# Low parts of the recurrence's weight slots: made by VectorE in whole slots instead of by GpSimd in pieces

## The chip, the cores and the metric

The kernel runs on one core of one Trainium2 chip. The metric is the device time of one execution in microseconds (us). Five engines matter here: TensorE (PE; its weight loads are listed apart as PEld), VectorE (DVE), ScalarE (ACT), GpSimd (POOL) and SyncE (SP), which issues most of the DMA.

## What is computed

The reference is one inference step of a decoder trunk of two layers over 512 prompt tokens and 8 sample tokens, all in fp32, with 1024 channels. Of a layer, this is what matters here:

```python
x = x + 0.5 * mod[:, :, 2] * _swiglu(pre(x, 0), ...)           # first FFN half step
h = pre(x, 1)
(u_pool, hq, hf, hi, hg, aq, ak, av, iq, ik, iw, gl) = _split_in(h @ P['w_in'][l])
ya, pool_new = _pool_mix(u_pool, ...)                          # branch A
f = lb + (1.0 - lb) * jax.nn.sigmoid(hf)
o_b, s_new = _hgrn_scan(hq, log(max(f, F_FLOOR)), 1.0 - f, hi, hgrn_prev[l])   # branch B, 4 heads of 128 x 64
yc = _dsa(q, qi, iw, pos, k_all, v_all, ki_all, n_sel)         # branch C, sparse attention
x = x + mod[:, :, 5] * (merged @ P['w_out'][l])
x = x + 0.5 * mod[:, :, 8] * _swiglu(pre(x, 2), ...)           # second FFN half step
```

Branch B is a gated linear recurrence. The kernel computes it exactly, per head, by a doubling scheme over blocks of 1, 2, 4 ... 128 tokens.

## The kernel before, in words

**Products in three parts.** Every fp32 weight product is made of three matmuls: a tensor is split into a high part (fp32r) and a low part (tensor minus high part), and `product` (L1863 to L1865) and `token_tile` (L2019 to L2021) issue high x high, low x high and high x low.

**Weight slots.** The weights arrive in slots of 128 x 2048 values (1 MB). There are two sets of buffers, j = 0 and 1; slot n uses set n % 2. Per slot SP loads `raw[j]` as soon as the low part of the slot two before it is made (it waits on `w_split[j]`; `load_mix`, L701). ScalarE copies `raw[j]` to `w_hi[j]` once TensorE is through with slot n - 2 (`head`, L877, which raises `head_split[j]`). Then GpSimd makes `w_lo[j] = raw[j] - w_hi[j]` in four pieces of 128 x 512 (`split`, L820), and the last piece raises `w_split[j]`. TensorE waits on `w_split[j]` before the slot's first matmul (`wait_slot`). GpSimd does this for every slot of the kernel, in order.

**The stage "mix".** After the first FFN half step each layer has a stage of twelve slots, in the order `u, hi, H0, aq0, H1, iq, H2, aq1, H3, kv, thin, hg` (the list `MIX`). H0 to H3 hold the query and forget weights of the recurrence's four heads; the others are the projections of the other branches, whose products TensorE does between the recurrence's own small steps. The stage `ga0` (gates) follows; GpSimd makes its slots too.

**The recurrence (`hgrn`, on TensorE, VectorE and ScalarE).** For each head hd = 0 to 3 there are eight levels n = 0 to 7 (`LEVELS` = 0, 1, 2, 4 ... 64). TensorE does, for each n: first one group of 24 matmuls of a weight slot as filling, then the level's eight small matmuls (L2165), for which it waits on `pair_ready`. The filling is, at n = 1 to 4, groups of the slot `BESIDE[hd]` (aq0, iq, aq1, kv); at n = 5 to 7 and ahead of the turned keys (`kbT`, L2178), the four groups of the next head's slot H(hd+1). In head 3 the slot `thin` is the filling at n = 5 and 6, and the slot `hg` at n = 7, ahead of `kbT` and after it.

VectorE does in `hgrn` per head: `start`, `finish` of the head before, `sample_columns`, `scores(hd, 0)`, and then for n = 0 to 6: `double(hd, n)`, which waits for level n + 1 of TensorE and scales `hk` (L1531) and `qm` (L1532; this one raises `pair_ready` for level n + 2, and after n = 6 for `kbT`) and `ends` (L1534); `scores(hd, n + 1)` (four masked copies, L1551) while n + 1 < 6; and for hd > 0 one step of the rotary embedding of the slot `BESIDE[hd - 1]` (`rotary_step`): step 0 is a sum (L1448), 1 and 2 are half-width products (L645, L647), 3 is a product of 1280 columns (L649), 4 a sum of 1280 columns (L651); steps 5 and 6 are empty. The order of VectorE's instructions is written out by hand; it waits in order.

In the code below `use`/`slot_use` number the slots, `link` makes VectorE wait for its own last instruction, and the level matmuls of TensorE are in `hgrn` under `@block.tensor`.

Of the kernel before, what the change touches and what calls it, by code (L numbers as in the profile page):

```python
# [23 lines left out]
F32 = mybir.dt.float32  # L24
# [4 lines left out]
ALU = mybir.AluOpType  # L29
# [78 lines left out]

MIX = ("u", "hi", "H0", "aq0", "H1", "iq", "H2", "aq1", "H3", "kv", "thin", "hg")
BESIDE = ("aq0", "iq", "aq1", "kv")  # L110
MIX_SOURCE = {n: SLOT0["token"] + i for i, n in enumerate(("u", "hi", "hg", "aq0", "aq1", "kv", "iq", "thin"))}
MIX_SOURCE.update({f"H{hd}": SLOT0["hgrn"] + hd for hd in range(HH)})
MIX_UNIT, _at = {}, 0
# [79 lines left out]
def x_updates(sub):  # L193

    return X_TILES * (sub // N_SUB) + (0, 2 * KT, 3 * KT)[sub % N_SUB]
# [100 lines left out]
def build(nc, d):  # L296

    ctx = ExitStack()
    with ctx:
# [3 lines left out]
        def sb(name, shape, dt=F32, at=None):  # L303
            size = 4 * int(np.prod(shape[1:]))
            if at is None:
                at = cursor[0]
                cursor[0] += -(-size // 32) * 32
            assert at + size <= 229368, (name, at + size)
            return nc.alloc_sbuf_tensor_at(name, list(shape), dt, offset=at)
# [6 lines left out]
        raw = [sb(f"raw{j}", [P, SLOT]) for j in range(2)]  # L316
        w_hi = [sb(f"w_hi{j}", [P, SLOT], F32R) for j in range(2)]
        w_lo = [sb(f"w_lo{j}", [P, SLOT], F32R) for j in range(2)]
# [156 lines left out]
        def sem(name):  # L475
            return ctx.enter_context(nc.semaphore(name))
# [6 lines left out]
        head_split = [sem(f"head_split{j}") for j in range(2)]  # L483
        w_split = [sem(f"w_split{j}") for j in range(2)]
# [96 lines left out]
        def slot_use(l, stage, r=0):  # L581

            return (LAYER_STREAM * l + STREAM0[stage]) // 2 + r
# [5 lines left out]
        def mix_unit(l, name, n=0):  # L589

            return main_unit(l, "mix", MIX_UNIT[name] + n)
# [5 lines left out]
        def wait_unit_taken(eng, unit):  # L597
            eng.wait_ge(main_taken[unit % 4], unit // 4 + 1 + PRIMED)
# [58 lines left out]
        def _(sp):  # L657
# [40 lines left out]
            def load_mix(l, slot):  # L698
                j = slot % 2
                sp.wait_ge(w_split[j], slot_use(l, "mix", slot // 2) + PRIMED)  # L700
                sp.dma_start(raw[j][:], d["w"][l * LAYER_SLOTS + MIX_SOURCE[MIX[slot]]]).then_inc(w_loaded[j], 16)  # L701

# [103 lines left out]
        @block.gpsimd  # L806
        def _(pool):
            for semaphore in primed:
                pool.sem_inc(semaphore, PRIMED)
            pool.memset(ones[:], 1.0).then_inc(setup_done, 1)  # L810
            pool.memset(h_hi[:, :, COLS:].bitcast(F32), 0.0).then_inc(setup_done, 1)
            pool.memset(h_lo[:, :, COLS:].bitcast(F32), 0.0).then_inc(setup_done, 1)

            def split(l, stage, r, j):
                n = COLUMNS[stage]

                pool.wait_ge(head_split[j], slot_use(l, stage, r) + 1)
                for first in range(0, n, SPLIT_PIECE):
                    cols = slice(first, min(n, first + SPLIT_PIECE))
                    last = pool.tensor_tensor(w_lo[j][:, cols], raw[j][:, cols], w_hi[j][:, cols].bitcast(F32),  # L820
                                              ALU.subtract)
                last.then_inc(w_split[j], 1)

            def square(sub, k):

                before = SQUARES * sub + 2 * k - 1
                if sub == 0:
                    if k == 0:
                        pool.wait_ge(x_loaded, 32)
                else:  # L830
                    pool.wait_ge(x_updated, x_updates(sub) - KT + k + 1)
                if k == 0:
                    pool.tensor_tensor(sq_sum[:], x[:, 0, :], x[:, 0, :], ALU.mult).then_inc(squared, 1)
                else:
                    pool.wait_ge(squared, before)
                    pool.tensor_tensor(sq[:], x[:, k, :], x[:, k, :], ALU.mult).then_inc(squared, 1)
                    pool.wait_ge(squared, before + 1)
                    pool.tensor_tensor(sq_sum[:], sq_sum[:], sq[:], ALU.add).then_inc(squared, 1)

            for k in range(KT):  # L840
                square(0, k)
            for l in range(DEPTH):
                for stage, slots, _ in STREAM:
                    sub = N_SUB * l + {"down01": 1, "out": 2, "down11": 3}.get(stage, 0)
                    if sub == N_SUB * l or sub == N_SUB * DEPTH:
                        with pool.Fori(0, slots // 2) as r:
                            for j in range(2):
                                split(l, stage, r, j)
                        continue
                    per = KT // slots  # L850
                    for slot in range(slots + 2):
                        if slot < slots:
                            split(l, stage, slot // 2, slot % 2)
                        for k in range(per * (slot - 2), per * (slot - 1)):
                            if k >= 0:
                                square(sub, k)
# [3 lines left out]
        def _(act):  # L860
# [207 lines left out]
            def hgrn(l):  # L1068
# [10 lines left out]
                act.wait_ge(pool_stored, 48 * (l + 1))  # L1079
                for hd, name in enumerate(BESIDE):  # L1080
                    if hd > 0:
# [192 lines left out]
        def _(dve):  # L1274
            v = nc.vector
# [3 lines left out]
            def bc(ap, shape):  # L1279
                return ap.to_broadcast(shape)  # L1280
# [164 lines left out]
            def square_sums(l, name, n, sq_):  # L1445
                dve.wait_ge(rot_squared, 4 * l + n)
                rows = rows_of[name] if name != "ki" else slice(14, 15)
                v.reduce_sum(rot_ms[:, 0, :, rows], sq_, axis=AX.X).then_inc(rot_reduced, 1)  # L1448

            def rotary_step(l, name, step):  # L1450

                if step == 0:
                    for u in range(3):
                        wait_unit_taken(dve, mix_unit(l, name, u))
                    if name != "iq":
                        square_sums(l, name, 1 if name == "aq0" else 2, rot_sq[:])
                else:
                    rotate(steps, step - 1, rot[:, :, rows_of[name], :], rot_tmp[:], rope if name == "iq" else rope_q)
# [37 lines left out]
            def hgrn(l):  # L1496
# [19 lines left out]
                def sample_columns(hd):  # L1516
# [2 lines left out]
                    v.tensor_copy(k_s[:, hd, :], hk[hd % 2][:, SEQ:COLS])  # L1519
                    link(v.tensor_copy(q_s[:, hd, :], hq[hd % 2][:, SEQ:COLS]))  # L1520

                def double(hd, n):


                    h = LEVELS[n + 1]
                    dve.wait_ge(side_full, SIDE[(l, "level", hd, h)] + 1)
                    m = SEQ // (2 * h)
                    ev = ends[n][:].rearrange("p (m a) -> p m a", a=2)
                    kv_ = hk[hd % 2][:, 0:SEQ].rearrange("p (m a h) -> p m a h", a=2, h=h)[:, :, 0, :]
                    qv = qm[hd % 2][:].rearrange("p (m a h) -> p m a h", a=2, h=h)[:, :, 1, :]  # L1530
                    v.tensor_tensor(kv_, kv_, bc(ev[:, :, 1:2], [P, m, h]), ALU.mult)  # L1531
                    v.tensor_tensor(qv, qv, bc(ev[:, :, 0:1], [P, m, h]), ALU.mult).then_inc(pair_ready, 1)  # L1532
                    pairs[0] += 1
                    link(v.tensor_tensor(ends[n + 1][:], ev[:, :, 0], ev[:, :, 1], ALU.mult))  # L1534
# [36 lines left out]
                for hd in range(HH):  # L1571
                    start(hd)
                    if hd > 0:
                        finish(hd - 1)
                    sample_columns(hd)
                    scores(hd, 0)
                    for n in range(len(LEVELS) - 1):
                        double(hd, n)
                        if n + 1 < MASKED:
                            scores(hd, n + 1)  # L1580
                        if hd > 0:
                            rotary_step(l, BESIDE[hd - 1], n)
                    link(v.tensor_copy(decay[:, hd % 2], ends[-1][:]))
                square_sums(l, "kv", 3, rot_sq[:, :, 0:2, :])
                finish(HH - 1)
# [260 lines left out]
        def _(pe):  # L1846
# [283 lines left out]
            def hgrn(l):  # L2130
# [18 lines left out]
                for hd in range(HH):  # L2149
                    for n, h in enumerate(LEVELS):  # L2150
                        if 1 <= n < 5 and hd + n > 1:
                            token_group(l, BESIDE[hd], n)
                        elif n >= 5 and hd + 1 < HH:
# [26 lines left out]
                    if hd + 1 < HH:  # L2180
                        token_group(l, BESIDE[hd + 1], 0)
                    else:
# [247 lines left out]
            for l in range(DEPTH):  # L2430
                for f in range(2):
# [7 lines left out]
                    if f == 0:  # L2439
# [6 lines left out]
                        pool_branch(l)  # L2446
                        token_group(l, BESIDE[0], 0)
                        pool_products(l)
                        token_group(l, BESIDE[0], 1)
                        hgrn(l)  # L2450
# [134 lines left out]
```

## Time and profile before

| | us |
|---|---|
| median of 3 runs | 2930.19 |
| lowest, highest run | 2920.36, 2930.44 |
| the profiled execution | 2916.29 |
| its span | 2914.5 |
| mean granted TensorE clock, share of 2.4 GHz | 0.967 |
| busy: TensorE, VectorE, ScalarE, GpSimd | 2740.3, 990.0, 817.3, 1116.9 |
| recurrence of layer 0, from the first level to the last head's `kbT` | about 551 to 695 |
| recurrence of layer 1 | about 1991 to 2135 |

The rows further down have times in us from the start of the span, unless they are marked ns. Busy times of TensorE are of pipelined matmuls, so a busy stretch says that it had work, not how fast that was: the pitch, the distance from one start to the next, says how fast. In a timeline each row has the start, the duration (of several instructions merged, from the first start to the last end), engine, line, operation, output<-inputs and shapes, the count, and in square brackets the idle time before it and what ended it.

### The profile page before, as it was taken

Reading aid. Unit: us, or ns where it says so; the run is one execution under the profiler, and the core shown is the slowest. Engines: PE = TensorE matmul, PEld = TensorE weight load, DVE = VectorE, ACT = ScalarE, POOL = GpSimd, SP = SyncE. Lnnn points to the kernel's source line nnn. Section 1 sums busy time; section 2 is a strip of 40 time slices with the busy share of each in tenths; the row PEclk is TensorE's granted clock in tenths of the full one; section 3 lists DMA queues with packets and bytes.
Section 4 is the critical chain, followed back from the end, with each engine's and each line's share of the span. In section 5 each row is a group of like instructions: output and inputs, shape, how many; then the busy total and the mean of one; then the engine's idle time right before and its main releaser. Section 6 shows DMA issues by size and latency. Waiting matters only on the chain.

```text
span 2914.5 us, 53187 instructions
## 1 busy us (share of the span) xinstructions
PE 2740.3 (94%) x21968; PEld 2576.9 (88%) x21968; DVE 990.0 (34%) x2372; ACT 817.3 (28%) x1250; POOL 1116.9 (38%) x897
## 2 busy tenths in 40 slices
PE   5999998999989989999979999989999899799998
PEld 2999997999878879999979999979988789799998
DVE  2111113267584441112131111134666844421121
ACT  1321222322344223212233212122233332232221
POOL 4434344333212254344444444442342123544443
PEclk7999998999999989999989999989999999899999
DMA  7334435212212223342224344441122122222322
GB/s 275 130 128 174 149 109 183 73 59 77 86 33 77 103 84 128 126 156 87 78 97 149 122 168 140 144 160 59 59 83 73 32 86 102 73 87 80 108 76 83
DMA packets 75223, 312.78 MB, mean 107 GB/s; under 512 B 14940, under 2 KB 25594, under 8 KB 57610
## 3 DMA queue, kind: packets, MB, share of 16 engines
q1 hardware_dynamic: 67394, 290.85, 29.3%
q10 hardware_dynamic: 7640, 19.17, 1.8%
q8 instruction: 147, 2.41, 0.3%
q14 instruction: 42, 0.34, 0.0%
HBM read 299.56 MB, written 10.66 MB: 106 GB/s over the span
## 4 chain that ended last, share of the span: by engine, by line
PE 89%; DVE 6%; issue 2%; ACT 1%; DMA 1%; SPq 0%; POOL 0%; DVEq 0%; ACTq 0%; POOLq 0%
PE bank L1863 23%; PE bank L1865 21%; PE bank L1864 21%; PE bank L2019 2%; PE bank L2020 2%; PE bank L2021 2%; PE bank L1897 2%; PE bank L2165 2%; PE bank L1931 2%; PE bank L1932 2%; PE bank L1933 2%; DMA ada_w<-in_ada 1%; PE bank L2285 1%; PE bank L2298 1%; DVE score L1649 1%
## 5 line engine op out<-in xcount | busy, mean ns | idle before, releaser
L820 POOL TENSOR_TENSOR w_lo<-raw,w_hi 128x512 fp32r<-128x512 f32 (+1 forms) x800 | 1010.6, 1295 | 1730.3 <-ACT w_hi L877 1730.3
L1863 PE MATMUL bank<-h_hi,w_hi 128*128 128x260 f32 x3744 | 1074.7, 287 | 3.5 <-ACT silu_g L913 3.5
L1864 PE MATMUL bank<-h_hi,w_lo 128*128 128x260 f32 x3744 | 1059.5, 283 | 0.0
L1865 PE MATMUL bank<-h_lo,w_hi 128*128 128x260 f32 x3744 | 1059.3, 283 | 0.0
L1863 PEld LDWEIGHTS bank<-h_hi,w_hi 128*128 128x128 f32 x3744 | 709.6, 190 | 54.7 <-issue 53.3
L1864 PEld LDWEIGHTS bank<-h_hi,w_lo 128*128 128x128 f32 x3744 | 709.8, 190 | 0.0
L1865 PEld LDWEIGHTS bank<-h_lo,w_hi 128*128 128x128 f32 x3744 | 709.5, 190 | 0.0
L877 ACT CAST w_hi<-raw 128x2048 fp32r<-128x2048 f32 (+3 forms) x220 | 377.9, 1718 | 547.5 <-PE bank L1865 472.2
L1863 PE MATMUL bank<-mid_hi,w_hi 128*128 128x260 f32 x1408 | 403.6, 287 | 9.8 <-DVE mid_lo L1379 9.8
L1865 PE MATMUL bank<-mid_lo,w_hi 128*128 128x260 f32 x1408 | 398.1, 283 | 0.0
L1864 PE MATMUL bank<-mid_hi,w_lo 128*128 128x260 f32 x1408 | 396.6, 282 | 0.0
L1374 DVE TENSOR_TENSOR prod<-silu_g,bank 128x260 f32<-128x260 f32 x176 | 74.9, 425 | 732.0 <-PE bank L1865 709.0
L1863 PEld LDWEIGHTS bank<-mid_hi,w_hi 128*128 128x128 f32 x1408 | 264.3, 188 | 30.3 <-issue 25.2
L1865 PEld LDWEIGHTS bank<-mid_lo,w_hi 128*128 128x128 f32 x1408 | 265.7, 189 | 0.0
L1864 PEld LDWEIGHTS bank<-mid_hi,w_lo 128*128 128x128 f32 x1408 | 265.4, 188 | 0.0
L916 ACT CAST mid_hi<-prod 128x260 f32 (+1 forms) x176 | 72.1, 410 | 487.0 <-DVE prod L1374 487.0
L1413 DVE SCALAR_TENSOR_TENSOR x<-bank,mod,x 128x260 f32 (+3 forms) x160 | 77.5, 485 | 296.2 <-PE bank L1865 248.1
L2019 PE MATMUL bank<-w_hi,h_hi 128*128 128x256 f32 x560 | 166.2, 297 | 7.9 <-DVE h_lo L1339 7.9
L2020 PE MATMUL bank<-w_hi,h_lo 128*128 128x256 f32 x560 | 161.7, 289 | 0.0
L2021 PE MATMUL bank<-w_lo,h_hi 128*128 128x256 f32 x560 | 161.6, 289 | 0.0
L1379 DVE TENSOR_TENSOR mid_lo<-prod,mid_hi 128x260 f32 (+1 forms) x176 | 102.6, 583 | 117.2 <-ACT mid_hi L916 117.2
L913 ACT ACTIVATE silu_g<-bank 128x260 f32<-128x260 f32 x176 | 68.2, 387 | 200.4 <-PE bank L1865 198.9
(321 smaller groups left out, 3224.5 us busy)
## 6 DMA issues: line engine op xcount, KB each, us to landing
raw<-in_w SPq DMA_DIRECT2D x120, 1024.0 KB, 4.9
ada_w<-in_ada SPq DMA_DIRECT2D x86, 768.0 KB, 4.4
raw<-in_w SPq DMA_DIRECT2D x64, 512.0 KB, 4.4
raw<-in_w SPq DMA_DIRECT2D x32, 768.0 KB, 4.5
raw<-in_w SPq DMA_DIRECT2D x32, 640.0 KB, 4.0
ada_first<-in_ada SPq DMA_DIRECT2D x10, 768.0 KB, 13.6
out_y<-x ACTq DMA_DIRECT2D x4, 1040.0 KB, 5.5
x<-out_y ACTq DMA_DIRECT2D x4, 1040.0 KB, 6.2
```

What stands on the lines that cost most here:

```text
L820: last = pool.tensor_tensor(w_lo[j][:, cols], raw[j][:, cols], w_hi[j][:, cols].bitcast(F32), ALU.subtract)
L877: s.copy(w_hi[j][:, 0:n], raw[j][:, 0:n]).then_inc(head_split[j], 1)
L916: s.copy(mid_hi[:, bass.ds(2 * r + j, 1), half(hf)].rearrange("p o n -> p (o n)"), prod[:, hf, :]).then_inc(mid_hi_ready, 1)
L1374: v.tensor_tensor(prod[:, hf, :], silu_g[:, hf, :], bank[2 * hf + 1][:, 0:HALF], ALU.mult).then_inc(main_taken[2 * hf + 1], 1)
L1379: v.tensor_tensor(mid_lo[:, at, half(hf)].rearrange("p o n -> p (o n)"), prod[:, hf, :], mid_hi[:, at, half(hf)].rearrange("p o n -> p (o ...
L1413: v.scalar_tensor_tensor(out=xs, in0=bank[b][:, 0:cols.stop - cols.start], scalar=md[:, bass.ds(at + 16, 1), 0:1].rearrange("p o c -> p (o ...
L1863: mm(out, wh(wb), xh(xb), start=(n == 0), stop=False)
L1864: mm(out, wl(wb), xh(xb), start=False, stop=False)
L1865: last = mm(out, wh(wb), xl(xb), start=False, stop=(n == len(blocks) - 1))
L2019: mm(out, h_hi[:, k, cols], w_hi[j][:, wcols], start=(k == 0), stop=False)
L2020: mm(out, h_lo[:, k, cols], w_hi[j][:, wcols], start=False, stop=False)
L2021: return mm(out, h_hi[:, k, cols], w_lo[j][:, wcols], start=False, stop=(k == KT - 1))
```

## The change

A constant `VECTOR_SPLITS = 4` is added. GpSimd makes the low parts of the first four slots of `mix` (u, hi, H0, aq0) as before, in pieces. The other eight (H1, iq, H2, aq1, H3, kv, thin, hg) are made by VectorE, each with one instruction of 128 x 2048: in head hd, slot 4 + 2 hd after the scores of n = 1, and slot 5 + 2 hd after `double` of n = 5. The rotary steps 0 to 4, which stood at n = 0 to 4, now stand at n = 0, 2, 3, 4 and 6.

```diff
+VECTOR_SPLITS = 4
...
             for l in range(DEPTH):
                 for stage, slots, _ in STREAM:
+                    if stage == "mix":
+                        for slot in range(VECTOR_SPLITS):
+                            split(l, stage, slot // 2, slot % 2)
+                        continue
                     sub = N_SUB * l + {"down01": 1, "out": 2, "down11": 3}.get(stage, 0)
...
+                def split(slot):
+
+                    j = slot % 2
+                    dve.wait_ge(head_split[j], slot_use(l, "mix", slot // 2) + 1)
+                    v.tensor_tensor(w_lo[j][:], raw[j][:], w_hi[j][:].bitcast(F32), ALU.subtract).then_inc(w_split[j], 1)
+
...
                         if n + 1 < MASKED:
                             scores(hd, n + 1)
-                        if hd > 0:
-                            rotary_step(l, BESIDE[hd - 1], n)
+                        if hd > 0 and n in (0, 2, 3, 4, 6):
+                            rotary_step(l, BESIDE[hd - 1], (0, 2, 3, 4, 6).index(n))
+                        if n in (1, 5):
+                            split(VECTOR_SPLITS + 2 * hd + n // 5)
```

## Rows read from the trace of the kernel before

**Rows 1.** The page: busy times, and the chain that ended last by engine.

```profile
PE 2740.3 (94%) x21968; PEld 2576.9 (88%) x21968; DVE 990.0 (34%) x2372; ACT 817.3 (28%) x1250; POOL 1116.9 (38%) x897
PE 89%; DVE 6%; issue 2%; ACT 1%; DMA 1%; SPq 0%; POOL 0%; DVEq 0%; ACTq 0%; POOLq 0%
```

**Rows 2.** Windows: one per head, layer 0; the last row head 3, layer 1.

```profile
core 0: us, PE busy (x) PEld busy (x) DVE busy (x) ACT busy (x) POOL busy (x), PEclk, DMA share, GB/s
553.00:586.00 33.00, 32.63 (x280) 32.47 (x280) 17.20 (x53) 8.64 (x13) 10.22 (x8) 1.00 0.10 33
586.00:623.00 37.00, 36.21 (x305) 35.69 (x305) 25.14 (x61) 8.43 (x14) 11.44 (x9) 1.00 0.17 58
623.00:661.00 38.00, 37.13 (x313) 36.61 (x313) 24.88 (x61) 9.79 (x16) 12.46 (x9) 1.00 0.16 56
661.00:698.00 37.00, 34.64 (x279) 34.14 (x277) 25.19 (x52) 10.20 (x19) 13.14 (x9) 0.95 0.26 87
...
2101.00:2138.00 37.00, 34.63 (x278) 34.12 (x278) 25.39 (x52) 10.37 (x19) 13.35 (x9) 0.95 0.28 87
```

**Rows 3.** Waits of TensorE, 550 to 712 us: total, times, longest.

```profile
PE bank L2165 <- DVE qm L1532: 3.3, 4, 1.9
PE bank L2141 <- issue: 1.1, 3, 0.4
```

**Rows 4.** Timeline of TensorE, head 3 of layer 0.

```profile
674.84 1.05 PE L2165 MATMUL bank<-qm,hk 128*128 128x128 f32 x8
...
678.59 1.05 PE L2165 MATMUL bank<-qm,hk 128*128 128x128 f32 x8
679.40 0.36 PE L1863 MATMUL bank<-h_hi,w_hi 128*68 128x260 f32 x1
...
683.01 1.13 PE L2165 MATMUL bank<-qm,hk 128*128 128x128 f32 x8 [0.49 <-DVE qm L1532]
684.05 0.39 PE L2019 MATMUL bank<-w_hi,h_hi 128*128 128x256 f32 x1
...
689.06 1.13 PE L2165 MATMUL bank<-qm,hk 128*128 128x128 f32 x8 [1.87 <-DVE qm L1532]
...
690.17 0.42 PE L2020 MATMUL bank<-w_hi,h_lo 128*128 128x256 f32 x1
...
693.38 0.35 PE L2020 MATMUL bank<-w_hi,h_lo 128*128 128x256 f32 x1
...
694.40 0.60 PE L2178 MATMUL bank<-ident,hk 128*128 128x128 f32 x4
```

**Rows 5.** Timeline of VectorE, head 3 of layer 0.

```profile
676.00 0.43 DVE L1531 TENSOR_TENSOR hk<-hk,ends 128x256 f32<-128x256 f32 x1 [1.48 <-PE bank L2165]
676.34 0.42 DVE L1532 TENSOR_TENSOR qm<-qm,ends 128x256 f32<-128x256 f32 x1
...
676.89 0.62 DVE L1551 COPY_PREDICATED att<-levels,bank 128x64 f32<-128x64 uint32 x4
677.43 2.57 DVE L649 TENSOR_TENSOR rot<-rot,rope_q 128x1280 f32<-128x1280 f32 x1
680.03 1.40 DVE L1531 TENSOR_TENSOR hk<-hk,ends 128x256 f32<-128x256 f32 x1
681.35 1.51 DVE L1532 TENSOR_TENSOR qm<-qm,ends 128x256 f32<-128x256 f32 x1
...
684.59 1.48 DVE L651 TENSOR_TENSOR rot<-rot,rot_tmp 128x1280 f32<-128x1280 f32 x1
```

**Rows 6.** Timeline of GpSimd: the slots aq1, hg and the first of `ga0`.

```profile
602.60 6.63 POOL L820 TENSOR_TENSOR w_lo<-raw,w_hi 128x512 fp32r<-128x512 f32 x4 [16.26 <-ACT w_hi L877]
...
677.36 6.64 POOL L820 TENSOR_TENSOR w_lo<-raw,w_hi 128x512 fp32r<-128x512 f32 x4 [16.32 <-ACT w_hi L877]
684.81 6.47 POOL L820 TENSOR_TENSOR w_lo<-raw,w_hi 128x512 fp32r<-128x512 f32 x4 [0.81 <-ACT w_hi L877]
```

**Rows 7.** Timeline of ScalarE: the high parts of `hg` and of `ga0`'s first slot.

```profile
675.36 1.92 ACT L877 CAST w_hi<-raw 128x2048 fp32r<-128x2048 f32 x1
...
682.83 1.90 ACT L877 CAST w_hi<-raw 128x2048 fp32r<-128x2048 f32 x1
```

**Rows 8.** One line of the program, L1513: ns minimum/median/maximum, first and last start.

```profile
L1513 DVE TENSOR_TENSOR qm<-hq,ends x8: 691/692/694, 551.6 to 2095.7; 128x512 f32<-128x512 f32 x8
```

**Rows 9.** Timeline of GpSimd: the slot H1, with VectorE idle beside it.

```profile
539.07 4.95 POOL L820 TENSOR_TENSOR w_lo<-raw,w_hi 128x512 fp32r<-128x512 f32 x4 [6.36 <-ACT w_hi L877]
```

**Rows 10.** DMA issues: KB each, median us from issue to landing.

```profile
raw<-in_w SPq DMA_DIRECT2D x120, 1024.0 KB, 4.9
```

**Rows 11.** Timeline of TensorE after the norm ahead of `mix`.

```profile
494.34 0.55 PE L2019 MATMUL bank<-w_hi,h_hi 128*128 128x256 f32 x1 [3.93 <-DVE h_lo L1339]
...
498.96 0.29 PE L2019 MATMUL bank<-w_hi,h_hi 128*128 128x256 f32 x1
```

## The prediction

> **What bounds the kernel now.** I read the page first: TensorE is busy 94% of the span and makes 89% of the chain that ended last, VectorE 6% [rows 1]. So a change on VectorE and GpSimd is worth only what TensorE's idle time and slow clock in the recurrence allow. Next come the windows, one per head. TensorE is busy 32.63 of 33, 36.21 of 37, 37.13 of 38 and 34.64 of 37 us; only in head 3 is its mean granted clock below full (0.95), and layer 1 repeats it (34.63 of 37, 0.95) [rows 2]. Summed, 4.4 us are idle per layer. The waits say on whom: 3.3 us in four waits on VectorE's `qm` (L1532), which releases a level, and 1.1 us in three waits for the chain of states, which the change does not touch [rows 3]. The waits of layer 1 read the same.
>
> The timelines say why. An undisturbed step from level to level takes 678.59 - 674.84 = 3.75 us: the level holds TensorE 679.40 - 678.59 = 0.81 us, the group of 24 matmuls 2.94 us [rows 4]. VectorE's `hk` starts 676.00 - 674.84 = 1.16 us after the level did. While GpSimd makes `hg` (677.36 to 684.00) and then `ga0`'s first slot (from 684.81) [rows 6], VectorE's steps stretch: `hk` from 0.43 to 1.40, `qm` from 0.42 to 1.51, the 1280-wide product takes 2.57 where a sum of that size takes 1.48 beside a gap of GpSimd [rows 5]. GpSimd pays too: 6.63 us for a slot [rows 6] against 4.95 with VectorE idle [rows 9]. Heads 1 and 2 have the same picture on a smaller scale (602.60 is head 1's).
>
> **What that costs now.** Head 3: from level 5 at 678.59, two steps to level 7 and one more to `kbT` would end at 678.59 + 3 x 3.75 = 689.84; `kbT` starts at 694.40 [rows 4]. That is 4.56 us: waits of 0.49 and 1.87; twice a slow restart (684.05 - 683.01 = 1.04 instead of 0.81, so 0.23 each); and the clock. From about 690 to 693.38 the matmul pitch is 0.21 us instead of 0.12 [rows 4], which is the lower level, 1.2 GHz; half of its 3.4 us, 1.6 with the edges, is lost. It set in after the two waits. Heads 1 and 2 have the other two waits, (3.3 - 2.36) / 2 = 0.47, and a restart: 0.7 each [rows 3, 4]. Sum: 4.56 + 1.4 = 5.9 us per layer. That, 11.9 us in the whole kernel, is the most that taking GpSimd away can return.
>
> **The change, part by part.** *Removed:* 8 slots x 4 pieces of GpSimd per layer, some 8 x 5 to 6.6 us of its time [rows 6, 9]. GpSimd is idle between slots, so this is worth nothing by itself; what counts is that VectorE is no longer slowed at n = 3 to 5 of heads 1 to 3. The waits of heads 1 and 2 go whole (1.4 us), and the 0.49 of head 3. Late next after them is nothing: `qm` ends 1.16 + 0.34 + 0.42 = 1.92 us after a level starts, 0.15 more reaches TensorE (681.35 + 1.51 to 683.01), and it is wanted at 3.75, so 1.7 us are to spare [rows 4, 5].
>
> *Added:* 8 instructions of 128 x 2048 on VectorE per layer. No row has this width. 512 columns take 0.69 us [rows 8], 1280 take 1.48 [rows 5], so 1.03 ns a column, and 2.27 us for 2048. The other end of what rows allow is GpSimd's pace for the same slot, 4.95 us [rows 9]. I take 2.27, since its row is of the same engine and operation; 4.95 makes a rival.
>
> *Splits at n = 1* (H1, H2, H3, thin). They stand after the masked copies, whose successor starts 677.43 - 674.84 = 2.6 us after the level [rows 4, 5]; plus 2.27 ends at 4.9, and the next `double` would start at 3.75 + 1.16 = 4.91. Cost nothing, covered by VectorE's idle time; if the cover is gone, 1.7 us more of slack stand behind it. TensorE wants these slots at n = 5, three steps later. The rotary product that moves to n = 4 ends at 2.6 + 1.48 = 4.1, the last sum at n = 6 stands beside neither scores nor a split: nothing too.
>
> *Splits at n = 5 of heads 0 to 2* (iq, aq1, kv). No scores there, so they run from 2.05 (1.16 for `hk`, 0.89 for the three products, as 676.00 to 676.89) to 4.32 after level 6. Their users come after `kbT`, over a step later. Nothing.
>
> *The split of `hg`, n = 5 of head 3.* This one is not covered. `double(3, 5)` waits for level 6, and TensorE's very next work after level 6 is the group of `hg`, which now waits for the split behind that `double`. GpSimd has hg's high part at 677.28 [rows 7] and would finish well before; VectorE holds it up by program order. With level 6 starting at T, TensorE is free at T + 0.81, and may start at T + 4.32 + 0.15 = T + 4.47: a new wait of 3.66 us, plus 0.23 of restart. With T = 678.59 + 3.75 = 682.34 the split starts at 684.39. ScalarE ends the high part of `ga0`'s first slot at 682.83 + 1.90 = 684.73 and GpSimd starts at 684.81 [rows 6, 7]: 0.4 us after the split, so the split is taken undisturbed. The nearer end is that, the farther one piece more, 4.95 / 4 = 1.24 us.
>
> *The clock.* Waits of 2.36 us brought 1.6 us of loss in head 3 [rows 4]; a pause of 3.93 after a mostly idle norm was followed by the lower level from 494.34 to 498.96, 2.3 us lost [rows 11]; nothing at all is the other end. One wait of 3.66 is nearest to the former: 1.6.
>
> *Queues.* SP loads a slot when the one two before is split. Those at n = 1 come later than GpSimd's, thin's near 672 instead of 661, so `ga0`'s first slot lands near 677 with 4.9 us of landing [rows 10]; ScalarE wants it at 682.83 [rows 7]. Nothing else is queued behind these loads on SP. The load behind `hg` moves from 684 to 687, and ScalarE wants it only after the last group of `hg`. GpSimd passes from aq0 to `ga0` and waits there.
>
> **Sum.** Lost per layer then: 3.66 + 0.23 + 1.6 = 5.5, against 5.9: 0.4 us better, 0.8 in two layers. The profiled execution's 2916.29 would become 2915.5; the median shown is 13.9 above it, so 2929.4. A gain at three places is paid back at a fourth.
>
> **A rule of the skill.** GpSimd's pieces and VectorE's products of two SBUF tensors stretch each other by about a piece [rows 5, 6]. The Trainium skill ("SBUF — State Buffer", the section on the engine and DMA sides) puts it as an exclusive lock: whoever starts first holds the shared port pair for the whole instruction. By that rule a 2048-wide split holds out longest, and a GpSimd piece that got in first would delay hg's split by its whole length. As a mechanism of this kernel that is the third case below.
>
> **The rivals.**
> 1. *Forecast:* as summed, 2929.4. Chance 0.55.
> 2. *The clock stays up in head 3*, since one wait replaces several: 3.9 lost instead of 5.5, 2.0 better per layer, 2926.2. For it: heads 1 and 2 wait without a fall. Against: their waits are under half a us. 0.20.
> 3. *GpSimd's piece of `ga0` gets in ahead of hg's split*, decided if ScalarE is 0.4 us earlier: 1.24 more, or the lower clock lasts as in [rows 11]. 6.7 lost, 0.8 worse per layer, 2931.8. 0.17.
> 4. *VectorE's wide split runs at GpSimd's pace, the one that ends slower.* At 4.95 us the splits at n = 1 end 2.6 + 4.95 - 4.91 - 1.7 = 0.9 late, four times; those at n = 5 0.4 late, three times; hg's wait grows by 2.7. In all 5.5 + 3.6 + 1.2 + 2.7 = 13.0 lost, 7.1 worse per layer, 2944.4. It turns to slower than before from 2.7 us per split. Against: both width rows lie on one line. 0.03.
> 5. *The stretching is not GpSimd's doing*, so the change does not do what it says: 5.9 stays and hg's 3.9 is added, 2938. Against: the long rows begin and end with GpSimd's. 0.03.
>
> 0.02 stays for what I do not see.
>
> **How the numbers follow.** Half a per cent, 14.7 us, is about what a measurement of this kernel can tell from no change. Cases 1 to 3 lie within it by far, and the runs shown spread over 10 us, mostly downwards from the median (2920.36, and the profiled 2916.29). The bound of 11.9 us excludes a gain over the half per cent by the mechanism alone. Faster 0.04, same 0.92, slower 0.04. The range takes cases 1 to 3 and the runs' spread: 2926.2 - 12 = 2914 to 2931.8 + 4 = 2936.
>
> **What the profile after should show.** VectorE `w_lo` x16 at 2.27 us; no wait on `qm` in heads 1 and 2; `hk` at 0.43 at n = 3 to 5; in head 3 a single wait of about 3.7 us on VectorE's `w_lo` ahead of `hg`'s first group, with the lower clock behind it; `kbT` of head 3 less than 2 us earlier than 694.40. It would be wrong if the hg wait were absent, if splits took over 2.7 us, or if another wait on `w_lo` appeared.

## The result, and the profile after

The changed kernel takes 2928.61 us in the median of 20 runs (2922.6 to 2935.2), the kernel before 2920.45 in the median of 20 (2916.34 to 2930.44). The ratio is 1.0021, with a 95% interval from 1.0012 to 1.0029: about 6 us slower, where 0.8 us faster was forecast. It is within the half per cent that had the chance of 0.92 and within the range, but on the other side. The three runs of before that were shown ahead of the prediction had a median of 2930.19; two of them were among the slowest of the twenty.

The page after, which answers to [rows 1], and the windows of the heads, which answer to [rows 2] (columns as there):

```profile
span 2927.9 us, 53095 instructions
PE 2751.5 (94%) x21968; PEld 2589.3 (88%) x21968; DVE 981.2 (34%) x2388; ACT 818.2 (28%) x1250; POOL 1026.1 (35%) x833
```

```profile
586.00:623.00 37.00, 36.63 (x313) 36.47 (x313) 23.99 (x62) 8.44 (x14) 0.00 (x0) 1.00 0.17 58
623.00:661.00 38.00, 37.63 (x321) 37.47 (x321) 23.41 (x62) 9.98 (x16) 0.00 (x0) 1.00 0.16 56
661.00:698.00 37.00, 33.67 (x266) 33.48 (x264) 20.61 (x50) 9.93 (x18) 6.71 (x4) 0.91 0.26 87
...
2101.00:2138.00 37.00, 32.96 (x279) 32.60 (x278) 21.50 (x57) 10.37 (x18) 7.07 (x4) 1.00 0.18 59
```

GpSimd is out of heads 1 and 2, and TensorE's idle time there falls from 0.79 and 0.87 us to 0.37, the wait for the chain of states, which stays. Head 3 is worse than before (33.67 instead of 34.64 busy, clock 0.91 instead of 0.95). Its timelines, TensorE and then VectorE and GpSimd, answer to [rows 4 to 6]:

```profile
681.06 1.05 PE L2178 MATMUL bank<-qm,hk 128*128 128x128 f32 x8
685.44 0.58 PE L2032 MATMUL bank<-w_hi,h_hi 128*128 128x256 f32 x1 [3.33 <-DVE w_lo L1531]
...
690.51 0.41 PE L2034 MATMUL bank<-w_lo,h_hi 128*128 128x256 f32 x1
690.73 1.20 PE L2178 MATMUL bank<-qm,hk 128*128 128x128 f32 x8
...
694.63 0.60 PE L2191 MATMUL bank<-ident,hk 128*128 128x128 f32 x4
```

```profile
682.22 0.43 DVE L1542 TENSOR_TENSOR hk<-hk,ends 128x256 f32<-128x256 f32 x1 [0.87 <-PE bank L2178]
682.56 0.42 DVE L1543 TENSOR_TENSOR qm<-qm,ends 128x256 f32<-128x256 f32 x1
682.89 0.16 DVE L1545 TENSOR_TENSOR ends<-ends 128x8 f32<-128x8 f32 x1
683.09 2.29 DVE L1531 TENSOR_TENSOR w_lo<-raw,w_hi 128x2048 fp32r<-128x2048 f32 x1
```

```profile
683.50 3.01 POOL L821 TENSOR_TENSOR w_lo<-raw,w_hi 128x512 fp32r<-128x512 f32 x1 [150.22 <-ACT w_hi L882]
```

The new wait is there, 3.33 us on VectorE's `w_lo`, ahead of the first group of `hg`; in layer 1 it is 3.67, since `hk` starts 1.51 us after the level there and not 1.16 (what held it is not shown). The split starts right behind the last product of `double(3, 5)` and takes 2.29 us; all sixteen take 2.29 to 2.32. `kbT` of head 3 starts at 694.63 instead of 694.40. In layer 0 the clock is at its lower level from the wait on up to the level at 690.73 (pitch 0.21 us); in layer 1 it stays up in this trace. GpSimd's first piece for `ga0` starts 0.41 us after the split and takes 3.01 us instead of some 1.27. In layer 1 GpSimd is only 0.06 us behind the split; there too the split takes 2.29 us:

```profile
2130.87 2.29 DVE L1531 TENSOR_TENSOR w_lo<-raw,w_hi 128x2048 fp32r<-128x2048 f32 x1
2130.93 7.12 POOL L821 TENSOR_TENSOR w_lo<-raw,w_hi 128x512 fp32r<-128x512 f32 x4 [150.21 <-ACT w_hi L882]
```

GpSimd's first piece takes 3.37 us this time. In both layers it ends 1.13 to 1.14 us behind the split. The Trainium skill's rule of the exclusive lock ("SBUF — State Buffer", the section on the engine and DMA sides) agrees: the one that starts first keeps its pace, and GpSimd's piece ends a little less than its own length after the split does.

So the recurrence, from its first level to the last `kbT`, takes 142.6 us in layer 0 and 140.5 in layer 1, against 142.9 twice. It is not slower. The 13.4 us between the two spans came up elsewhere, in stages that hold the same instructions in both kernels. The busy times say of what kind they are: TensorE's 21968 matmuls are busy 2740.3 us before [rows 1] and 2751.5 after, 11.2 of the 13.4 us; only 2.2 are idle time. The same matmuls ran at a lower granted clock (0.967 over the span before, 0.964 after). The plainest place is behind the recurrence. Windows of 706 to 715 us, the kernel before first, then the changed one:

```profile
706.00:709.00 3.00, 3.00 (x18) 2.34 (x16) 2.16 (x3) 1.87 (x5) 2.20 (x2) 1.00 0.15 48
709.00:712.00 3.00, 3.00 (x25) 2.95 (x25) 2.93 (x3) 0.00 (x0) 3.00 (x3) 1.00 0.28 83
712.00:715.00 3.00, 3.00 (x27) 2.87 (x25) 2.86 (x5) 0.39 (x1) 0.70 (x1) 1.00 0.42 79
```

```profile
706.00:709.00 3.00, 3.00 (x18) 2.51 (x18) 1.93 (x3) 2.10 (x5) 1.97 (x2) 0.85 0.13 43
709.00:712.00 3.00, 3.00 (x11) 2.25 (x10) 2.93 (x3) 0.00 (x0) 3.00 (x3) 0.50 0.34 91
712.00:715.00 3.00, 3.00 (x16) 3.00 (x15) 2.86 (x5) 0.00 (x0) 0.88 (x1) 0.51 0.37 85
```

TensorE is busy in both; in the second it runs at 1.2 GHz for nearly 7 us. What it does before the fall is the same: the outputs of head 3, `thin_turn` and the twelve small matmuls of `i_bcast` (contraction over 8 rows), which begin within 0.23 us of each other:

```profile
706.27 2.85 PE L2225 MATMUL bank<-h_i,row_select 8*128 8x256 f32 x12
```

```profile
706.50 3.97 PE L2238 MATMUL bank<-h_i,row_select 8*128 8x256 f32 x12
```

An FFN shows it too, behind a short wait on `mid_lo` that both kernels have. The kernel before goes on at a pitch of 0.12 us, the changed one falls to 0.22:

```profile
1423.93 0.38 PE L1863 MATMUL bank<-mid_hi,w_hi 128*128 128x260 f32 x1 [1.75 <-DVE mid_lo L1379]
...
1425.11 0.29 PE L1863 MATMUL bank<-mid_hi,w_hi 128*128 128x260 f32 x1
1425.23 0.28 PE L1864 MATMUL bank<-mid_hi,w_lo 128*128 128x260 f32 x1
```

```profile
1430.49 0.38 PE L1876 MATMUL bank<-mid_hi,w_hi 128*128 128x260 f32 x1 [1.75 <-DVE mid_lo L1384]
...
1431.84 0.42 PE L1877 MATMUL bank<-mid_hi,w_lo 128*128 128x260 f32 x1
1432.06 0.42 PE L1878 MATMUL bank<-mid_lo,w_hi 128*128 128x260 f32 x1
```

The last FFN of the changed kernel has two more such falls, which the kernel before has not (its clock is 1.00 at both places):

```profile
2672.00:2680.00 8.00, 6.22 (x40) 6.02 (x39) 0.86 (x2) 1.78 (x2) 3.75 (x3) 0.79 0.10 13
2860.00:2867.00 7.00, 6.39 (x40) 6.39 (x41) 0.79 (x2) 0.93 (x1) 3.22 (x3) 0.76 0.22 56
```

### The profile page after: what moved, and what is told of

Its sections match the earlier page's. It is cut to its first block, busy times and chain, and to the rows that moved or that the text cites. A ratio compares the mean times of both kernels' runs of the same rounds, so it can differ in the third digit from the quotient of the medians.

```text
span 2927.9 us, 53095 instructions
## 1 busy us (share of the span) xinstructions
PE 2751.5 (94%) x21968; PEld 2589.3 (88%) x21968; DVE 981.2 (34%) x2388; ACT 818.2 (28%) x1250; POOL 1026.1 (35%) x833
## 4 chain that ended last, share of the span: by engine, by line
PE 90%; DVE 5%; ACT 1%; issue 1%; DMA 1%; POOL 0%; SPq 0%; DVEq 0%; ACTq 0%; POOLq 0%
PE bank L1876 23%; PE bank L1878 22%; PE bank L1877 22%; PE bank L2032 2%; PE bank L2033 2%; PE bank L2034 2%; PE bank L1910 2%; PE bank L2178 2%; PE bank L1944 2%; PE bank L1945 2%; PE bank L1946 2%; PE bank L2298 1%; PE bank L2311 1%; DVE score L1662 1%; DMA ada_first<-in_ada 1%
## 5 line engine op out<-in xcount | busy, mean ns | idle before, releaser
L821 POOL TENSOR_TENSOR w_lo<-raw,w_hi 128x512 fp32r<-128x512 f32 (+1 forms) x736 | 919.8, 1282 | 1834.5 <-ACT w_hi L882 1834.5
L2032 PEld LDWEIGHTS bank<-w_hi,h_hi 128*128 128x128 f32 x560 | 110.5, 197 | 15.5 <-issue 8.0
```

What stands on the lines that cost most here:

```text
L2032: mm(out, h_hi[:, k, cols], w_hi[j][:, wcols], start=(k == 0), stop=False)
```

## The experiments

A fall, below, is a stretch in which TensorE's granted clock is at its lower level, 1.2 GHz. The theories: A, the wait on hg's split ate the gain; B, the loss comes from falls of the clock in later stages and has nothing to do with hg. After e1 to e4 two more: C, a shift of the work by a few us or less decides which of the later pauses is followed by a fall; D, the later stages are a constant and gains and losses add. Ratios are to the kernel before on the same chip, with their 95% intervals. e1 to e4, e9, e10, b0 and a0 ran on one chip, e5 to e8 on a second, b1, b2, a1 and c1 on a third.

**e1: hg's split one step earlier, before level 6 is waited for; the rotary product goes to n = 5.**

```diff
-                        if hd > 0 and n in (0, 2, 3, 4, 6):
-                            rotary_step(l, BESIDE[hd - 1], (0, 2, 3, 4, 6).index(n))
-                        if n in (1, 5):
-                            split(VECTOR_SPLITS + 2 * hd + n // 5)
+                        late = 4 if hd == HH - 1 else 5
+                        turns = (0, 2, 3, 9 - late, 6)
+                        if hd > 0 and n in turns:
+                            rotary_step(l, BESIDE[hd - 1], turns.index(n))
+                        if n in (1, late):
+                            split(VECTOR_SPLITS + 2 * hd + (n > 1))
```

> Theory A (the wait on hg's split in head 3, with the lower clock behind it, is what ate the gain): with the split one step earlier the wait of 3.3 to 3.7 us is gone, kbT of head 3 in layer 0 comes near 689 instead of 694.4, and the whole kernel is 10 to 12 us faster than before (ratio 0.996 to 0.997). Theory B (the loss comes from clock falls in later stages that the recurrence has no part in): the wait is gone but the time stays at the changed kernel's, ratio 1.000 to 1.002.

Measured: 2916.37 us in the median, ratio 0.9989 (0.9979 to 0.9998). Head 3 in both layers, windows, and `kbT`:

```profile
661.00:692.00 31.00, 30.91 (x264) 30.72 (x262) 23.21 (x50) 9.94 (x18) 6.24 (x4) 1.00 0.27 87
2101.00:2132.00 31.00, 30.91 (x263) 30.72 (x262) 23.21 (x50) 9.94 (x18) 6.24 (x4) 1.00 0.25 84
```

```profile
688.16 0.60 PE L2193 MATMUL bank<-ident,hk 128*128 128x128 f32 x4
```

No wait but the one for the states is left, the clock is up, and the recurrence takes 136.9 us in both layers: 6.0 less than before, 5.7 and 3.6 less than in the changed kernel. Twice 6.0 us are won there, and 3.2 us arrive at the end (0.6 to 6.1 by the interval). Neither theory's range holds: A foresaw 0.996 to 0.997, B 1.000 to 1.002. Against the changed kernel e1 wins 9.3 us in the recurrence and 9.3 in the ratios, but that they agree proves nothing, since the stages behind differ too, as the traces further down show.

**e2: GpSimd makes hg, VectorE the other seven.**

```diff
-                        for slot in range(VECTOR_SPLITS):
+                        for slot in (*range(VECTOR_SPLITS), 11):
...
-                        if n in (1, 5):
+                        if n in (1, 5) and (hd, n) != (HH - 1, 5):
```

> GpSimd makes hg, VectorE the other seven. Theory A: no wait on w_lo; the stretching comes back in head 3 alone, at n = 3 and 4, for a wait on qm of 0 to 0.5 us; ratio to before 0.996 to 0.998. Theory B: 1.000 to 1.002, as in the changed kernel.

Measured: 2925.39 us, ratio 1.0015 (1.0003 to 1.0026). The recurrence is 140.4 and 140.5 us, 2.5 better than before, with one wait on `qm` of 1.9 us in head 3, so the stretching in head 3 costs more than the 0 to 0.5 expected. And yet the whole is slower, within B's range and outside A's. The recurrence in this trace is as long as the changed kernel's in layer 1, and it has no wait on hg: that wait alone is not what makes the whole slower.

**e3: the kernel before, with the low parts of the eight slots made by nobody.** This leaves part of the computation out.

```diff
+                    if stage == "mix":
+                        for slot in range(slots):
+                            if slot < 4:
+                                split(l, stage, slot // 2, slot % 2)
+                            else:
+                                pool.wait_ge(head_split[slot % 2], slot_use(l, stage, slot // 2) + 1)
+                                pool.sem_inc(w_split[slot % 2], 1)
+                        continue
```

> The kernel before, with the low parts of the eight slots left out (nobody makes them, the semaphore is raised at once): part of the computation is missing, so its time is a bound only. If GpSimd's pieces are what stretches VectorE's steps: hk and qm at 0.43 us throughout heads 1 to 3 up to ga0's split, no wait on qm in heads 1 and 2, about 11 us faster than before (ratio 0.996). If they are not: the long rows and the four waits stay, ratio 1.000.

Measured: 2917.78 us, ratio 0.9989 (0.9977 to 1.0002). The windows of heads 1 to 3:

```profile
586.00:623.00 37.00, 36.63 (x314) 36.47 (x312) 19.49 (x60) 8.44 (x14) 0.00 (x0) 1.00 0.19 62
623.00:661.00 38.00, 37.63 (x322) 37.47 (x321) 18.91 (x60) 9.99 (x16) 0.00 (x0) 1.00 0.18 56
661.00:698.00 37.00, 36.69 (x312) 36.49 (x311) 19.64 (x53) 10.64 (x19) 5.21 (x4) 1.00 0.18 59
```

The recurrence takes 137.0 us in both layers, 5.9 less. GpSimd's pieces are what stretches VectorE, shown by taking them away. But this kernel too, with 11.8 us less in the recurrence, ends only some 3 us earlier where 11 were expected, and its interval reaches 1.

**e4: the kernel before, with only the rotary steps moved.**

```diff
-                        if hd > 0:
-                            rotary_step(l, BESIDE[hd - 1], n)
+                        if hd > 0 and n in (0, 2, 3, 4, 6):
+                            rotary_step(l, BESIDE[hd - 1], (0, 2, 3, 4, 6).index(n))
```

> The kernel before with the rotary steps at the changed kernel's places, the splits on GpSimd. If the move of the steps has a part in the gain of heads 1 and 2: their waits on qm shrink. I expect the opposite: the 1280-wide product now stands at n = 4, behind three stretched steps, so the waits move to level 7 and grow, to 0.5 to 0.8 us in heads 1 and 2 and 3 to 4 us in head 3; ratio 1.000 to 1.002.

Measured: 2918.5 us, ratio 0.9990 (0.9979 to 1.0002), and against my expectation 139.5 us in the recurrence, 3.5 less than before. Waits of TensorE, 550 to 699 us, and the product where it now stands:

```profile
PE bank L2165 <- DVE qm L1532: 1.9, 1, 1.9
```

```profile
676.07 1.92 DVE L647 TENSOR_TENSOR rot_tmp<-rot,rope_q 128x640 f32<-128x640 f32 x1
...
682.59 1.49 DVE L649 TENSOR_TENSOR rot<-rot,rope_q 128x1280 f32<-128x1280 f32 x1
```

One wait is left of four, and no fall follows it. While GpSimd works on hg, VectorE now has the half-width step beside it (1.92 us where the wide product took 2.57), and the wide one comes when GpSimd is between two slots (1.49). So more than half of what the eight splits were to win can be had in the recurrence without moving any of them; for the whole kernel no gain is shown, the interval reaches 1. The changed kernel has both, the moved steps and the moved splits, and in heads 1 and 2 either alone ends the waits (e3, e4).

**e5 to e10: the same kernels, shifted.** To shift the later stages by a known amount, 6 to 28 matmuls of a slot that is there anyway are put ahead of the last groups of `hg`; TensorE stays busy at its usual pitch of 0.12 us, and the product is overwritten.

```diff
+            def more_matmuls(l, count):
+                out = bank[mix_unit(l, "hg", 1) % 4][:, 256:512]
+                for n in range(count):
+                    mm(out, h_hi[:, n % KT, 3 * P:4 * P], w_hi[1][:, n % KT * 256:(n % KT + 1) * 256],
+                       start=(n == 0), stop=(n == count - 1))
...
+                more_matmuls(l, 12)
                 token_group(l, "hg", 3)
                 token_group(l, "hg", 4)
```

e5 and e6 are e1 with 12 and 21:

> The version with hg's split one step earlier, and 12 repeated matmuls per layer (1.44 us of busy TensorE at 0.12 us each) ahead of the last groups of hg; their product is overwritten. Theory C (a shift of a few us decides which of the short pauses of the later stages are followed by the lower clock): the time does not move by 2 x 1.44 us but by steps, as the falls near 703, 765, 976 and 1424 us go or stay; anything from 4 us faster to 6 us slower than without them. Theory D (the time behind the recurrence is a constant, gains and losses add): exactly 2.9 us slower, ratio 0.9999 to before.

> The same with 21 repeated matmuls per layer (2.5 us). That puts the end of the recurrence about 3.5 us ahead of the kernel before, where the version with only the rotary steps moved stood, which had no fall from 693 to 780 us. Theory C: the falls near 703 and 765 us are absent in the trace and the time is no worse than without the repeated matmuls (ratio 0.998 to 0.999). Theory D: 5.0 us slower, ratio 1.0006.

e7 is the changed kernel with 24, e8 the kernel before with 12:

> The changed kernel with 24 repeated matmuls per layer (2.9 us). Theory C: the falls at 708 and 773 us of the changed kernel go or move, and the time changes by less than half of the 5.8 us of added work, or falls; ratio to before 0.999 to 1.003. Theory D: 5.8 us slower than the changed kernel, ratio 1.0041.

> The kernel before with 12 repeated matmuls per layer (1.44 us). Theory C: shifted by 1.4 us it gets falls near 708 and 772 us which it did not have, and is slower by more than the added work, 5 to 9 us, ratio 1.002 to 1.003. Theory D: 2.9 us slower, ratio 1.001.

e9 and e10 are the kernel before with 28 and 6:

> The kernel before with 28 repeated matmuls per layer (28 x 0.12 = 3.4 us), that is one length of a short fall. So far the stretch from the first i_bcast matmul to the first yab matmul took 64.1 to 64.2 us where that matmul started 224.1, 224.3, 227.5 and 227.8 us behind the fall of the norm ahead of mix, and 65.9 to 67.6 in all other traces. Theory C: at 227.6 + 3.4 = 231.0 the position is favourable again, that stretch takes 64.2, and the whole is slower by the added work alone, 6.8 us, ratio 1.0023 - less than the 7.9 us that 2.9 us of added work cost (e8). Theory E (any added work in this place has its own surcharge): 10 to 19 us slower, ratio 1.0035 to 1.0065.

> The kernel before with 6 repeated matmuls per layer (0.7 us). Theory C: 0.7 us is enough to leave the favourable position (228.3 us; 228.1 took 65.9): the same stretch takes 65.9 or more, and 1.4 us of added work cost 4 to 8 us, ratio 1.0014 to 1.0027. Theory D (gains and losses add): 1.4 us, ratio 1.0005.

| | matmuls added, us in both layers | ratio to before (95%) | if it added, ratio |
|---|---|---|---|
| e1 | 0 | 0.9989 (0.9979 to 0.9998) | |
| e5 | 2.9 | 0.9989 (0.9976 to 1.0003) | 0.9999 |
| e6 | 5.0 | 0.9986 (0.9973 to 0.9999) | 1.0006 |
| changed | 0 | 1.0021 (1.0012 to 1.0029) | |
| e7 | 5.8 | 1.0033 (1.0018 to 1.0047) | 1.0041 |
| e10 | 1.4 | 1.0020 (1.0008 to 1.0031) | 1.0005 |
| e8 | 2.9 | 1.0027 (1.0011 to 1.0042) | 1.0010 |
| e9 | 6.8 | 1.0020 (1.0009 to 1.0031) | 1.0023 |

Five us of added work cost e1 nothing that can be measured, and 1.4 us cost the kernel before at least 2.3. D fails at e6, e8 and e10, where the additive value lies outside the interval, though at e8 only by 0.0001 and at e6 with an interval of its own around the value it starts from; at e5, e7 and e9 it lies inside, and they decide nothing between C and D. Theory E, a surcharge for any added work in this place, is out by e9 (1.0020 where it wanted at least 1.0035). C is what is left, but it does not say beforehand which way a shift goes: e6 was to be free of the falls near 705 and 770 in both layers, and was so in layer 1 alone. Its windows at `i_bcast`, layer 0 and then layer 1:

```profile
707.00:712.00 5.00, 5.00 (x23) 4.50 (x22) 4.79 (x7) 0.00 (x0) 2.95 (x2) 0.51 0.29 64
...
2151.00:2155.00 4.00, 4.00 (x36) 4.00 (x36) 3.86 (x5) 0.39 (x1) 3.24 (x2) 1.00 0.13 47
```

How narrow the favourable positions are comes out when the traces are put side by side. The distance is taken from where the lower clock of the norm ahead of `mix` ends (498.96 in [rows 11]) to the first `i_bcast` matmul; beside it stands how long the work from there to the first `yab` matmul took. The expectations of e9 and e10 count from where that lower clock starts, 20.5 us earlier.

| distance, us | stretches | i_bcast to yab, us |
|---|---|---|
| 201.1 to 201.6 | e1, e3, c1, both layers | 66.0 to 66.1 |
| 202.6 to 203.3 | e5, both layers; e6, layer 0 | 67.4 to 67.6 |
| 203.6 to 203.8 | e4, both layers; e6, layer 1 | 64.1 to 64.2 |
| 204.4 to 205.3 | changed and a0, layer 1; e2, both layers; b0, layer 0 | 65.9 to 66.0 |
| 206.3 to 206.9 | changed and a0, layer 0; a1, both layers; b0, layer 1 | 67.5 to 67.7 |
| 207.1 to 207.3 | before, b1, b2, both layers | 64.1 to 64.2 |
| 207.6 to 208.8 | e10, e8, both layers; e7, layer 0 | 65.7 to 66.0 |
| 209.7 to 210.8 | e9, both layers; e7, layer 1 | 65.6 to 67.6 |

These are all 36 stretches of the eighteen traces, those of the unchanged kernels further down included, and the work is the same in each. Every stretch in two narrow bands takes 64.1 to 64.2 us, whatever the kernel, and none outside them does. b0 is the kernel before: at 206.92 it takes 67.7 us, where b1, the same kernel, takes 64.1 at 207.07. So the length goes with the position and not with the kernel. The changed kernel's recurrence, 0.3 us shorter in layer 0 and 2.5 in layer 1, puts it at 206.6 and 204.7 us, outside the bands. e9 was to come back to 64.2 and did not: at 210.8 and 210.2 it took 65.6 and 67.6; whether a third band exists is not shown.

The FFN of layer 0 (from its norm to the next layer's first norm) sorts in the same way. Here the distance is from where the lower clock of that norm ends to the first matmul behind the wait on `mid_lo` shown above:

| distance, us | traces | lower clock behind the wait | FFN, us |
|---|---|---|---|
| 336.7 to 336.8 | changed, a0, a1, b2, e1, e5, e6 | yes | 421.0 to 421.1 |
| 337.4 to 337.5 | c1, e2, e8, e10 | yes | 419.1 to 419.2 |
| 337.4 to 337.5 | b0, e9 | no | 417.6 |
| 337.8 to 337.9 | before, b1, e3, e4, e7 | no | 418.5 to 418.6 |

The middle rows show that the distance alone, to a tenth of a us, does not always decide.

**The unchanged kernels again.** Each b is the kernel before, each a the changed one, c1 is e1.

> The kernel before, unchanged, for another trace. Theory C with a position that is the kernel's own: recurrence 142.9 us in both layers, stretch from i_bcast to yab 64.1 to 64.2. If the position differs from execution to execution, that stretch may take 65.9 or 67.6 and the span 2920 to 2930.

> The changed kernel, unchanged, for another trace. If the position is the kernel's own: recurrence 142.6 and 140.5 us, stretch to yab 67.6 and 66.0. If it differs from execution to execution, these vary by one or two steps of 1.7 us.

> The kernel before, unchanged. If the surcharge in the FFN stages is the changed kernel's own: from the second norm of layer 0 to the first of layer 1 417.6 to 418.6 us, and from the last norm to the end 406.6 to 406.8, as in both traces so far. If it is the execution's: 421 or 411.6 appears here too.

> As b1; the stages of the gates and of the attention are expected to differ between b1 and b2 by steps of 1.7 us (64 to 68, 224 to 232), since the two traces so far did.

> The changed kernel, unchanged. If the surcharge is the kernel's own: 421.0 and 411.6 us in the two FFN stages, recurrence 142.6 and 140.5, span 2927 to 2929. If it is the execution's: 418.5 or 406.7 appears.

> The version with hg's split one step earlier, unchanged: recurrence 136.9 us in both layers whatever the execution; FFN stages 421.0 and 407.6 if they are the kernel's own.

Lengths in us, both layers added, from the starts of the first matmuls of each stage in the traces (`yab` and `yc` are the outputs of branches A and B, and of C, where the first matmuls read them; FFN: from the last norm of each layer up to the next layer's first norm, or the end):

| trace | span | recurrence | i_bcast to yab | yab to yc (attention) | FFN |
|---|---|---|---|---|---|
| before | 2914.5 | 285.9 | 128.3 | 448.4 | 825.3 |
| b0 | 2932.9 | 284.4 | 133.7 | 462.8 | 824.3 |
| b1 | 2912.9 | 285.9 | 128.3 | 448.0 | 826.1 |
| b2 | 2919.1 | 285.9 | 128.3 | 449.3 | 828.6 |
| changed | 2927.9 | 283.1 | 133.6 | 451.5 | 832.6 |
| a0 | 2928.3 | 283.1 | 133.6 | 451.6 | 832.6 |
| a1 | 2930.3 | 284.6 | 135.2 | 453.9 | 828.6 |
| e1 | 2914.5 | 273.9 | 132.0 | 453.9 | 828.6 |
| c1 | 2916.8 | 273.9 | 132.0 | 457.4 | 827.7 |

The recurrence is the kernel's own to 1.5 us. What comes behind differs from execution to execution, most in the attention (448 to 463 for the very same kernel before, 18 to 20 us in the span between b0 and the two fastest; b0's execution, 2934.66 us, is slower than all 23 others of its kernel on that chip, 2917.3 to 2930.8). The surcharge in the FFNs is the execution's too: 421.0 us in layer 0 appears in b2, and of the changed kernel's two surcharges the second, 411.5 us, is absent in a1 (407.5). But it is not chance alone: in three of four traces the kernel before has the short 128.3, and neither the changed kernel nor e1 ever has it. Means, changed minus before: recurrence -1.9, i_bcast to yab +4.5, attention +0.2, FFN +5.2, together +8.0; the medians of twenty runs differ by 8.2, the ratio says 6. Without b0 the attention alone would say +3.8 instead of +0.2, so how the loss is shared out among the stages is rough. e1 minus before: -11.6, +2.4, +3.5, +2.0, together -3.7; its ratio says -3.2. In the same means TensorE's busy time is 4.7 us longer in the changed kernel, for the same matmuls, and its idle time 4.3; the clock accounts for the first part, what makes the idle time longer is not shown.

## Why the prediction was wrong, point by point

- **The split's price.** 2.27 us from the width rows; 2.29 to 2.32 measured. GpSimd's pace (4.95), the rival that was to end slower, is ruled out.
- **The covered splits.** At n = 1 and n = 5 of heads 0 to 2 they cost nothing: no wait on `w_lo` but hg's, one in each layer.
- **The end of the stretching.** Foreseen to end the waits of heads 1 and 2 and one in head 3: so it is. But the moved rotary steps alone do as much (e4), a gain that the prediction did not count. The bound on what GpSimd's absence returns, 5.9 us per layer, was measured twice, 5.9 in e3 and 6.0 in e1.
- **The wait on hg.** 3.66 forecast; 3.33 and 3.67. GpSimd did start behind the split, so the third case did not arise, but the 0.4 us it was to be behind held in layer 0 alone; in layer 1 they were 0.06.
- **The clock in head 3.** 1.6 us was taken for each layer, the value after waits of 2.36. Against e1, which has neither wait nor fall, the changed kernel loses 5.7 us in layer 0 of all three traces, 3.33 of them the wait, so 2.3 for the clock and the restart (6.8 us at the lower level, 1.2 of them inside the wait); in layer 1 it loses 3.6, all wait, in two traces, and 1.5 more than the wait in the third. The mean, 1.4, is near the forecast's 1.6 + 0.23; the single falls were not foreseen.
- **The sum of the recurrence.** 0.4 us better per layer forecast, 0.95 measured in the mean over the traces.
- **The step that failed** is the last one of the sum, which was nowhere written as a step: "The profiled execution's 2916.29 would become 2915.5". It takes a gain or loss in the recurrence as one of the whole. The bound was put just so: "11.9 us in the whole kernel, is the most that taking GpSimd away can return". e1 and e3 reach 12 us in the recurrence and return 3. The changed kernel wins 1.9 there and loses 9.9 behind, in the means of the traces, where its later pauses and thin stretches more often stand where the clock falls after them. The prediction looked at the clock only beside the waits it changed, and put the rest at nothing without a reason.
- **The median.** The forecast was laid on the median of the three runs, 2930.19; the kernel before has 2920.45 over twenty. The predicted time, 2929.4, is close to the measured 2928.61 by luck: the base was 9.7 us too high, and the 8 us that the later stages lost were not foreseen.

What is shown: the waits and their sizes, GpSimd as the cause of the stretching, that the later stages grow and shrink with no change in them, and that their length goes with their position, which a shift of 0.7 us per layer (e10) or chance (b0) moves. What stays open: why one execution of a kernel comes to stand elsewhere than the next (the changed kernel has 832.6 in the FFNs in two of three traces and 828.6 in the third), where the added idle time comes from, and whether another chip would sort the kernels otherwise. The ratio of 1.0021 belongs to this kernel as a whole, not to the idea.

Of the complete versions, hg's split one step earlier (e1, 0.9989) and the same with 21 matmuls added (e6, 0.9986) have an interval clear of 1; they cannot be told from each other, nor from moving the rotary steps alone (e4, 0.9990).

## What to carry to other kernels

A whole-slot operation put on another engine "at a fixed level" is free only where its user is later than the next event that the engine waits for; list each user's own deadline, as for hg, and move the one split that misses it. Before moving work off an engine that disturbs another, try the order alone: here it gave 3.5 of 6 us per layer in the recurrence. And where a kernel keeps TensorE 94% busy, a gain of a few us must be judged over many runs, since the same later stages vary by more than that.

## What the runs showed of the hardware

- The clock falls with TensorE busy 3.00 of 3.00 us and no wait listed, during matmuls whose contraction is over 8 rows (changed kernel, 706 to 712 us); and at distances of 207.07 and 206.92 us, 0.15 us apart in two executions of one kernel (b1, b0), the following work takes 64.1 or 67.7 us.
- Behind one and the same wait of 1.75 to 1.78 us the clock falls for 3.4 us in eleven traces and stays up in seven (the FFN of layer 0).
- Adding 5 us of full matmuls did not make a kernel measurably slower (e6); adding 1.4 us made another one about 6 us slower (e10).
- A 128 x 2048 subtraction on VectorE takes 2.29 us and is not disturbed by GpSimd when it starts first, be it by 0.06 us; a 128 x 512 piece on GpSimd that starts 0.41 or 0.06 us later takes 3.01 or 3.37 us instead of 1.27.
- One and the same kernel had spans from 2912.9 to 2932.9 us in four traces, with the recurrence alike to 1.5 us.
